# Inputs on another queue, a rotation one head later, and three products placed earlier in a two-model fp32 kernel

## The reference, cut to what matters

```python
h = rmsnorm(x, ln1_g)
cq, ckv, k_rope, sb_q, sb_k, sb_v, df_q, df_k, df_v, gates = split(h @ w_in)
mla = softmax_attention(...)          # branch 0: 8 heads, 64 wide values
sb  = stick_breaking_attention(...)   # branch 1: 8 heads of 64
q, k = rope(rmsnorm(df_q)), rope(rmsnorm(df_k))
df  = differential_attention(q, k, df_v)   # branch 2: 4 double heads
df  = rmsnorm(df) * g
g0, g1, g2 = split(sigmoid(gates + gate_b))
x = x + (g0 * (mla @ w0) + g1 * (sb @ w1) + g2 * (df @ w2)) @ w_out
x = x + relu(rmsnorm(x) @ w_ff1) ** 2 @ w_ff2
```

## Time and profile before

| what | value |
|---|---|
| median of 3 runs | 2835.17 us (2826.72 to 2835.69) |
| the profiled execution's own time | 2834.15 us |
| its span | 2832.8 us |
| TensorE busy | 2706.9 us (96%) |
| VectorE busy | 1043.1 us (37%) |
| ScalarE busy | 500.7 us (18%) |
| mean granted TensorE clock | 0.979 of 2.4 GHz |
| chain that ended last | TensorE 90%, VectorE 5%, ScalarE 2%, DMA 2% |

### The profile page before, as it was taken

The page is one execution under the profiler, slowest core; times in us unless marked ns, Lnnn a source line. Parts: engine busy times, 40 slices in busy tenths (PEclk is TensorE's granted clock), DMA queues, the critical chain, the costliest instruction groups (busy, mean ns, idle before and its releaser), DMA issues.

```text
span 2832.8 us, 41965 instructions
## 1 busy us (share of the span) xinstructions
PE 2706.9 (96%) x16738; PEld 1941.5 (69%) x16738; DVE 1043.1 (37%) x2381; ACT 500.7 (18%) x1088; POOL 102.7 (4%) x98
## 2 busy tenths in 40 slices
PE   7998899999998899999999999999999899999998
PEld 5776678887776788878855555555888755555554
DVE  2555323333555323322334222223563353222223
ACT  2322301001222211001311111111333111111112
POOL 0000000000000000000010000000000010000000
PEclk9999999999999999999999999999999899999999
DMA  5132246563232357655359999996322479999995
GB/s 201 60 120 90 89 151 249 223 278 120 90 120 89 113 198 267 268 193 218 117 229 405 415 412 418 409 415 265 119 91 73 166 314 418 411 419 413 407 403 208
DMA packets 104994, 684.63 MB, mean 242 GB/s; under 512 B 17760, under 2 KB 19312, under 8 KB 24496
## 3 DMA queue, kind: packets, MB, share of 16 engines
q1 hardware_dynamic: 93040, 665.02, 59.5%
q0 software_dynamic: 11264, 16.54, 1.7%
q10 hardware_dynamic: 576, 1.43, 0.1%
HBM read 703.37 MB, written 4.19 MB: 250 GB/s over the span
## 4 chain that ended last, share of the span: by engine, by line
PE 90%; DVE 5%; ACT 2%; DMA 2%; issue 1%; ACTq 0%; SPq 0%; DVEq 0%
PE PS L491 85%; PE PS L496 5%; DMA wmoe<-in_experts 1%; ACT AR L2279 1%; ACT AR L2329 1%; DMA COLS<-in_cols 0%; DVE ST L1428 0%; DVE AR L1425 0%; ACT ST L2279 0%; DVE AR L1597 0%; ACT wmoe L2279 0%; DVE AR L1595 0%; DVE AR L1436 0%; DVE AR L1572 0%; ACT X L2279 0%
## 5 line engine op out<-in xcount | busy, mean ns | idle before, releaser
L491 PE MATMUL PS<-H,wdense 128*128 128x256 f32 (+1 forms) x3056 | 703.0, 390 | 9.4 <-DVE H L1460 3.5
L491 PEld LDWEIGHTS PS<-H,wdense 128*128 128x128 f32 x3056 | 580.6, 192 | 115.2 <-issue 13.7
L2279 ACT ACTIVATE AR<-PS 128x256 f32<-128x256 f32 (+7 forms) x515 | 229.0, 451 | 1505.2 <-PE PS L491 938.1
L491 PE MATMUL PS<-wmoe,AR 128*64 128x256 f32 (+2 forms) x3248 | 470.0, 444 | 5.9 <-issue 3.3
L491 PE MATMUL PS<-AR,wdense 128*128 128x256 f32 (+1 forms) x1920 | 435.1, 387 | 7.1 <-DVE AR L1647 2.9
L491 PEld LDWEIGHTS PS<-AR,wdense 128*128 128x128 f32 x1920 | 367.1, 191 | 71.3 <-issue 3.7
L491 PE MATMUL PS<-AR 128*128 128x512 f32 (+16 forms) x1604 | 370.4, 392 | 30.5 <-DVE AR L1436 12.9
L491 PEld LDWEIGHTS PS<-wmoe,AR 128*64 128x64 f32 (+1 forms) x3248 | 226.5, 137 | 206.5 <-issue 127.4
L491 PE MATMUL PS<-wdense,AR 128*64 128x256 f32 (+3 forms) x2384 | 287.5, 385 | 0.6 <-DVE AR L2136 0.5
L491 PEld LDWEIGHTS PS<-AR 128*128 128x128 f32 (+6 forms) x1604 | 189.2, 183 | 121.5 <-issue 85.1
L491 PEld LDWEIGHTS PS<-wdense,AR 128*64 128x64 f32 (+2 forms) x2384 | 175.4, 138 | 100.3 <-issue 18.5
(11 more groups left out here) (276 smaller groups left out, 1284.9 us busy)
## 6 DMA issues: line engine op xcount, KB each, us to landing
wmoe<-in_experts SPq DMA_DIRECT2D x262, 1024.0 KB, 11.0
wdense<-in_dense SPq DMA_DIRECT2D x176, 1024.0 KB, 4.8
wdense<-in_experts SPq DMA_DIRECT2D x140, 1024.0 KB, 13.9
wmoe<-in_ada SPq DMA_DIRECT2D x48, 1024.0 KB, 7.0
tokens<-AR POOLq DMA_DIRECT2D x4, 512.0 KB, 2.9
wdense<-in_dense SPq DMA_DIRECT2D x2, 768.0 KB, 10.6
wdense<-in_dense SPq DMA_DIRECT2D x2, 640.0 KB, 6.3
CST<-in_const SPq DMA_DIRECT2D x1, 1197.0 KB, 19.4
```

What stands on the lines that cost most here:

```text
L491: return te.matmul(out, lhsT, rhs, start=start, stop=stop, skip_group_check=True)
L2279: return ac.activation(dst, src, f, bias=bias, scale=scale)
```

## The change

Three edits, the second and third in both layers of the first block.

1. The two loads of X are issued by SyncE's queue, ahead of the first weights. ScalarE's queue issues the ones and COLS alone, each with a semaphore of its own. TensorE waits for the ones alone; ScalarE for COLS, after its squares; VectorE for both.
2. The third step of `rope_dk` moves from the seventh pass of the stick-breaking loop to the eighth, behind two products of the gates. VectorE then copies the transposed probabilities of the sixth head ahead of it.
3. Products 0 and 1 of branch 0 are made in the fourth pass of the double-head loop, between the gates' product and `turn_probs`; product 2 behind the loop, ahead of the wait for `o squared`. Their banks are held until the four column sums have their own.

```diff
-    BESIDE_MLA, BESIDE_SB, BESIDE_DF = (2, 1, 1, 1, 1, 1, 1, 1, 1), (4, 4, 4, 4, 4, 5, 5, 6, 6), (2, 2, 2, 1, 1)
+    BESIDE_MLA, BESIDE_SB, BESIDE_DF = (2, 1, 1, 1, 1, 1, 1, 1, 1), (4, 4, 4, 4, 4, 5, 4, 7, 6), (2, 2, 2, 1, 1)
...
-                           (dv, 1), (rope_dk, 1), (gate, 2), (dqt, 4), (gate, 2), (dkt, 4))
+                           (dv, 1), (gate, 2), (rope_dk, 1), (dqt, 4), (gate, 2), (dkt, 4))
...
+            def branch_steps(br):
+                for s in range(2):
+                    slot, use = take(4, 512), uses[0] - 1
+                    for j in range(4):
+                        what = ("branch", L, br, 4 * s + j)
+                        o = bank(what, VE)
+                        PE.up(sum_k(o[:, lo:T], [slot[:, k, j * P:(j + 1) * P] for k in range(4)],
+                                    [BR[:, 4 * br + k, lo:T] for k in range(4)]), *what)
+                        if j == 3:
+                            used(use)
+                        yield
+            branches = [branch_steps(br) for br in range(3)]
+            def ahead(*columns):
+                te.wait_ge(VE.sem, VE.of("mla out", L, 3))
+                for c in columns:
+                    advance(branches[0], 1)
+                    held.append(bank_of[("branch", L, 0, c)])
...
                 advance(gate, BESIDE_DF[h])
+                if h == DF_H - 1:
+                    ahead(0, 1)
                 if h > 0:
...
+            ahead(2)
             te.wait_ge(AC.sem, AC.of("o squared", L))
             for h in range(DF_H):
                 column_sums(("o square sums", L, h), [WORK[:, T * h:T * (h + 1)]], T)
+            held.clear()
...
-        te.wait_ge(first_loads, 32)
+        te.wait_ge(ones_load, 16)
...
-        ac.dma_start(CST[:, 0:2 * P], io["const"][:, 0:2 * P]).then_inc(first_loads, 16)
-        for j in range(2):
-            ac.dma_start(X[:, 4 * j:4 * j + 4, :], io["xT"][:, 4 * j:4 * j + 4, :]).then_inc(x_loads[j], 16)
-        ac.dma_start(COLS[:], io["cols"]).then_inc(first_loads, 16)
+        ac.dma_start(CST[:, 0:2 * P], io["const"][:, 0:2 * P]).then_inc(ones_load, 16)
+        ac.dma_start(COLS[:], io["cols"]).then_inc(cols_load, 16)
...
+            for j in range(2):
+                sp.dma_start(X[:, 4 * j:4 * j + 4, :], io["xT"][:, 4 * j:4 * j + 4, :]).then_inc(x_loads[j], 16)
             load(2)
```

More of the change, by code:

```diff
@@ L257, in build @@
     x_loads = [nc.alloc_semaphore(f"x_loaded{j}") for j in range(2)]
-    first_loads, table_loads, later_loads = [nc.alloc_semaphore(n) for n in ("first_loads", "table_loads", "later_loads")]
+    ones_load, cols_load = nc.alloc_semaphore("ones_loaded"), nc.alloc_semaphore("cols_loaded")
+    table_loads, later_loads = nc.alloc_semaphore("table_loads"), nc.alloc_semaphore("later_loads")
     dense = Ring(WD, 4, [nc.alloc_semaphore(f"dense_landed{s}") for s in range(4)])
@@ L755, in first_layer @@
                     te.wait_ge(VE.sem, VE.of("o normed", L))
[L756 to L763, removed]
+                run(branches[br])
             te.wait_ge(VE.sem, VE.of("merged", L))
@@ L2249, in vector_program @@
         VE.up(ve.memset(EPSC[:, 3:4], 0.0), "eps")
-        ve.wait_ge(first_loads, 32)
+        ve.wait_ge(ones_load, 16)
+        ve.wait_ge(cols_load, 16)
         for L in range(DEPTH):
@@ L2775, in scalar_program @@
             AC.up(act(SQX[:, 4 * j:4 * j + 4, :], X[:, 4 * j:4 * j + 4, :], Square), "x squared", j)
-        ac.wait_ge(first_loads, 32)
+        ac.wait_ge(cols_load, 16)
         for L in range(DEPTH):
```

## The result

The changed kernel takes 2802.28 us, median of 4 runs (2801.38 to 2810.84), beside 2834.52 for before on the same chip. The ratio is 0.990, with an interval of 0.988 to 0.992, so 23 to 34 us are gained. The profiled execution took 2802.76 with a span of 2801.4.

A forecast was written before the change was run, and what follows sets the result against it. TensorE, busy 96% of the span, was taken as the bound. Gains of 9.8 + 11.4 + 2.4 = 23.6 us off 2834.15 gave 2810.6, and 2811.5 with the 1.0 to the median; range 2800 to 2822.

The forecast's parts named there:

- Start: Kernel start: X ahead of the weights lets TensorE begin at about 6.3 instead of 16.14, gaining 9.8 us, bounds 4.3 and 10.5.
- The price by the first slot's place in the queue: Start: X, taking the first weights' place in SyncE's queue, lands at about 5.0 and 6.8 us.
- Rotation: Seventh stick-breaking pass, both layers: moving six VectorE operations later gains 2 × 5.68 = 11.4 us, bounds 8 and 15.
- the clock: Behind the shortened seventh-pass stops: no gain from the clock level, bounds -2 and +2 us for each layer.
- Products ahead: Double heads to branches: three early products gain 2.4 us in layer 0, 0 in layer 1, with a new bank wait; bounds -3 and +6.
- the rival with the free bank: Behind the column sums: product 3's bank is free, so no stop; 17.9 us gained for 2.4, 2796 us, chance 0.06.
- Sum: Whole kernel: 23.6 us gained and carried to the end, 2810.6 us, or 2811.5 with the 1.0 to the median.
- X no sooner: Start: X lands no earlier than before, so 4.3 us is gained for 9.8, giving 2817 us; chance 0.12.
- the delayed keys: Stick-breaking loop: the moved rotation delays a bank or the keys, a new wait of up to 9 us, 2820; chance 0.06.
- the uncarried gain: Kernel end: the experts' weights set the end, so the gain is made but not carried, 2834 us; chance 0.04.
- the slow branch stage: Branch products 3 to 23, both layers: the bank wait leaves TensorE at its lower clock throughout, fully 2886 us; chance 0.02.

The follow-up runs named there:

- edit 1 alone: Changed kernel with the rotation's move and the three products ahead undone, leaving X ahead of the weights: 2822.91 us against 2830.66 for before, ratio 0.998.
- edit 2 alone: Before with only the keys' rotation moved one head later: 2816.13 us, 14.5 us less than before, ratio 0.996.
- banks held longer: Changed kernel with the three banks held until the first branch is done: 2789.57 us, 17.8 us below the changed kernel, ratio to before 0.985.
- the first comparison: Changed kernel, all three edits, against before on the same chip: 2802.28 us beside 2834.52, ratio 0.990.
- both comparisons: Changed kernel, all three edits, measured twice against before: 2802.28 us, then 2807.36 us, ratio 0.990 each time.
- the semaphores alone: Before with separate semaphores for the start's loads, X still on ScalarE's queue: 2826.05 us, 4.6 us less than before, ratio 0.999.
- the norm's second step later: Changed kernel with the second step of the keys' norm moved to the eighth pass: 2797.15 us, 10.2 us below the changed kernel, ratio to before 0.988.

## Why the prediction was right, step by step

**Start.** Right. Forecast: first matmul at 6.3, gain 9.8. Measured: 6.48, and 9.3 at the first weights' product; edit 1 alone gave 10.5 there, 8.9 at the start of the rest and 7.8 in the medians. The price by the first slot's place in the queue held: X at 5.1 and 6.9 for 5.0 and 6.8. The Trainium skill (DMA: Bandwidth & Descriptors, Anatomy of one DMA) gives its fit for transfers that GpSimd issues; the estimate from it, 6.0 for the second half, was 0.9 us too early for SyncE's queue. The split into 4.6 for COLS and some 4.8 for X, which the bounds of this part stood on, was measured by the run with X left on ScalarE's queue. That the sums run at the lower level is read from their durations alone: the clock records of before begin at 21.4 us. What I did not foresee is a fall of the clock at 29.4 us in this profile (last section), which costs 3.3 of the 9.3; a shorter stretch of lower clock behind the stop at 118 us gives back 1.7.

**Rotation.** The mechanism was right to a tenth: stops of 2.20 and 3.18 for 2.2 and 3.2, the rotation from 241.4 behind the gate copy, the keys' transposes without a wait. The cover is real but small: one pass further TensorE waits 2.6 and 2.8. The term that was mis-sized is the clock, which I took at nothing with -2 and +2 as its bounds in each layer. Layer 0 gave 7.9 for 5.7 and layer 1 4.8: 12.7 for 11.4, and 12.4 with edit 2 alone. In layer 0 the clock stayed up behind the 2.2 us stop; in layer 1, behind 3.18, it fell and the gain was 0.9 below the stop's. The stop of 2.0 us that I set against a gain from the clock (123.7 to 125.7) is not in this loop, as I wrote, but in the first attention's.

**Products ahead.** Right, in its sum and in each part: 2.9 and -0.2 for 2.4 and 0, new stops of 5.71 and 5.49, product 3 at 7.8 us behind the sums' start for 7.6. Alone the edit gave 2.1 and -0.2 in the profile and 0.6 us in the medians. That the bank was the cause, only argued before, is shown: with the banks held longer the two stretches gain 10.6 and 7.6, 18.2 us, where the rival with the free bank had reckoned 17.9 from the rows. The bank rival was thus right on the price and wrong on the kernel as changed.

**Sum.** 23.6 forecast up to the rest, 23.4 and 24.6 found there in the two profiles of the changed kernel; the three edits singly make 8.9 + 10.2 + 2.1 = 21.2, and the clock fell in different places in each. That part was no luck. What the forecast lacked is a spread for everything behind: "What follows the first block starts off its last product, so the 23.6 carries to the end" holds, but the rest itself is 1766 to 1781 us long by chance, and I took it as the profiled execution had it. That execution lay at 2834, on the slow side of before, whose 29 runs have a median of 2830.7. So the first comparison came out 9 us below the point of 2811.5 and 2 us from the edge of the range, the second 4 us below the point; how near to the edge it fell was chance. Against the 0.990 of both comparisons, 28 us, the forecast is some 5 us short, and at the low edge of both intervals (23 to 34). The profiles show no such shortfall ahead of the rest, so it is spread or stays open.

**Rivals.** X no sooner, the delayed keys, the uncarried gain and the slow branch stage: none came. Behind the stops of 5.71 and 5.49 us the clock cost 1.8 and 2.2 us, not a stage. My reason for this, that the clock was back within 5 us after every stop, does not agree with its rows: behind the stop that ends at 125.7 the clock is still at 0.50 in 129.0 to 132.5, and it is back at 134.0, 8 us on. The price of that rival, 2886, comes to 2888 with the 21.2 named beside it.

## What to carry to other kernels

Before work is moved ahead into a stop, follow the buffers it takes until their reader comes: three banks taken early were wanted back before VectorE could read them, and the edit was worth 1 to 2 us until the banks were held past that point, then some 15 more. When an engine is late, look at what stands in its queue ahead of the one small copy that others wait for, and move whatever has cover elsewhere; reckon the cover to the next user and try one place too far to know it. And compare a stretch that no edit touches in both profiles before a gain is believed: here it moved by up to 15 us, and the time at which it begins is a steadier measure of the edits ahead of it than the median of the whole.

## What the runs showed of the hardware

The lower clock level came while TensorE was busy. In the changed kernel TensorE stood for 1.83 us ahead of 15.12 and was busy from there on, with 48 rows 32 columns wide from 26.3, and at 29.4 the granted clock went to 0.50 for 6.8 us while it stayed busy (start:end, length, TensorE busy and count, weight loads, VectorE, ScalarE, GpSimd, clock, DMA share, GB/s):

```profile
26.30:29.40 3.10, 3.10 (x40) 3.05 (x39) 0.55 (x2) 0.00 (x0) 0.00 (x0) 1.00 0.02 5
29.40:36.20 6.80, 6.80 (x22) 5.64 (x22) 0.38 (x3) 0.00 (x0) 0.00 (x0) 0.50 0.45 154
```

The kernel with edit 1 alone ran the same products at 25 to 38 us at 1.00 throughout, and before did too:

```profile
25.00:38.00 13.00, 13.00 (x87) 11.24 (x86) 1.84 (x7) 1.93 (x5) 0.00 (x0) 1.00 0.24 86
```

This fall stands in 4 of the 12 profiles (the changed kernel, edit 2 alone, the semaphores alone, the norm's second step later). They are the four in which the eight sums at the very start took longest, 6.8 to 7.0 us beside 5.5 to 6.5 in the others.

The same stop is not always answered in the same way. A stop of 2.06 us in the first attention of layer 0 was followed by a stretch at 0.50 in all 12 profiles, for 3.4 us in the four just named and for 6.8 in the other eight. A stop of 1.7 us in the first attention of layer 1 was followed by one in 4 of the 12. The stop of 2.2 us in the seventh pass of layer 0 was followed by none in any of the 5 profiles that have it. With the stops of 7.9 and 8.9 us came 10.2 us at 0.50, beginning inside them, in every profile that has them. One and the same kernel differs by 15 us in one stretch, nearly all of it from such falls. What decides it within a program is not settled by these runs.
